# Three PEER stages: score tiles behind the key products and into the gates, wide one-hot compares on VectorE, the weight multiplied in by GpSimd

## The reference

```python
def block(xt):
    q = (xt @ w_q).reshape(T, PEER_HEADS, 2, PEER_HALF)
    s = jnp.einsum('thpd,hpkd->thpk', q, sub_keys)
    s_top, i_top = lax.top_k(s, PEER_TOPK)
    cand = s_top[:, :, 0, :, None] + s_top[:, :, 1, None, :]
    cand_id = i_top[:, :, 0, :, None] * PEER_NKEYS + i_top[:, :, 1, None, :]
    best, pos = lax.top_k(cand, PEER_TOPK)
    eid = jnp.take_along_axis(cand_id, pos, axis=-1)
    gate = jax.nn.softmax(best, axis=-1)
    act = gelu(jnp.einsum('td,thkd->thk', xt, u_tab[eid]))
    return jnp.einsum('thk,thkd->td', gate * act, v_tab[eid])
```

## Time and profile before

| | |
|---|---|
| median of 3 runs | 4071.81 us (4068.31 to 4077.5) |
| the profiled execution, its own time | 4068.67 us |
| its span in the profile | 4066.9 us |
| TensorE busy (modelled) | 87% |
| VectorE, ScalarE, GpSimd busy | 57%, 34%, 11% |
| mean granted TensorE clock | 0.921 of full speed |

### The profile page before, as it was taken

How to read it: one execution, slowest core, us unless ns; L and a number is a source line. 1 busy time by engine, 2 the same in 40 slices (tenths; PEclk the granted TensorE clock), 3 DMA queues, 4 the chain that set the end, 5 groups by cost and what they waited for, 6 DMA issues and landing times. The chain is left out here.

```text
span 4066.9 us, 58259 instructions
## 1 busy us (share of the span) xinstructions
PE 3554.5 (87%) x20168; PEld 2950.0 (73%) x20168; DVE 2324.1 (57%) x4790; ACT 1370.9 (34%) x2097; POOL 427.4 (11%) x460
## 2 busy tenths in 40 slices
PE   7888999999866879999999748797678789999996
PEld 3677899999733667999999627575336779999993
DVE  1488666666314688666666263433205886666662
ACT  1136444444110246444444111111202464444442
POOL 0156000000000274000000000000001650000000
PEclk9999999999987999999999857677789999999998
DMA  4311555555330412555555300000134125555552
GB/s 182 146 57 53 186 186 186 186 187 188 135 127 11 151 52 79 190 186 186 187 187 187 114 0 1 1 1 25 53 118 150 53 69 190 186 186 186 186 186 95
DMA packets 126699, 511.64 MB, mean 126 GB/s; under 512 B 14704, under 2 KB 15344, under 8 KB 119152
## 3 DMA queue, kind: packets, MB, share of 16 engines
q1 hardware_dynamic: 126576, 510.07, 35.0%
HBM read 508.96 MB, written 1.05 MB: 125 GB/s over the span
## 5 line engine op out<-in xcount | busy, mean ns | idle before, releaser
L381 PE MATMUL ps<-xh,uhigh 128*128 128x256 f32 x3072 | 870.5, 283 | 14.7 <-POOL ulow L763 14.7
L383 PE MATMUL ps<-xh,ulow 128*128 128x256 f32 x3072 | 869.2, 283 | 0.0
L382 PE MATMUL ps<-xl,uhigh 128*128 128x256 f32 x3072 | 869.1, 283 | 0.0
L381 PEld LDWEIGHTS ps<-xh,uhigh 128*128 128x128 f32 x3072 | 588.1, 191 | 32.7 <-POOL ulow L763 19.8
L382 PEld LDWEIGHTS ps<-xl,uhigh 128*128 128x128 f32 x3072 | 588.2, 191 | 13.0
L383 PEld LDWEIGHTS ps<-xh,ulow 128*128 128x128 f32 x3072 | 588.1, 191 | 0.0
L728 DVE TENSOR_TENSOR ulow<-stream,uhigh 128x1024 fp32r<-128x1024 f32 x330 | 404.4, 1225 | 184.7 <-ACT uhigh L506 175.1
L506 ACT CAST uhigh<-stream 128x1024 fp32r<-128x1024 f32 x336 | 353.0, 1051 | 413.6 <-DMA stream<-in_u 413.6
L399 PE MATMUL ps<-vhigh,chigh 128*128 128x512 f32 x1536 | 479.7, 394 | 1.8 <-DVE vlow L744 1.5
L399 PE MATMUL ps<-vlow,chigh 128*128 128x512 f32 x1536 | 475.9, 391 | 0.0
L399 PE MATMUL ps<-vhigh,clow 128*128 128x512 f32 x1536 | 474.5, 390 | 0.0
(11 more groups left out here) (347 smaller groups left out, 4050.7 us busy)
## 6 DMA issues: line engine op xcount, KB each, us to landing
stream<-in_u SPq DMA_DIRECT2D x384, 512.0 KB, 4.0
stream<-in_v SPq DMA_DIRECT2D x369, 512.0 KB, 3.3
big<-in_wq SPq DMA_DIRECT2D x24, 1152.0 KB, 7.6
stream<-in_ab_w_in SPq DMA_DIRECT2D x4, 2048.0 KB, 9.1
stream<-in_c_w_qf SPq DMA_DIRECT2D x16, 512.0 KB, 3.4
stream<-in_c_w_ig SPq DMA_DIRECT2D x4, 2048.0 KB, 7.8
stream<-in_w_gates SPq DMA_DIRECT2D x4, 2048.0 KB, 8.3
spare<-in_v SPq DMA_DIRECT2D x15, 512.0 KB, 3.3
```

The lines of the kernel that those rows point to most:

```text
L381: pe.matmul(out, uh[:, b, cols], c.xh[:, k, :], start=k == 0, stop=False)
L382: pe.matmul(out, uh[:, b, cols], c.xl[:, k, :], start=False, stop=False)
L383: ins = pe.matmul(out, ul[:, b, cols], c.xh[:, k, :], start=False, stop=k == KD - 1)
```

## The change

HELD stays 16; EARLY = 24 score tiles are now made ahead of the loop, and the loop has STEPS = 104. Lines of the changed kernel are given as the diff has them.

- *Selection*: four score tiles after round 1's key products, two after round 2's, none after round 3's, ten after the residual product. GpSimd's picks now stand ahead of the low halves of the same round.
- *Gates*: VectorE makes A for two quads with one compare without the weight (128x1024), and B for two quads (128x1024) or, every other time, for one (128x512); ScalarE makes B of every fourth quad. GpSimd multiplies the weight into A of every quad (one tensor_tensor of 128x512) and makes no B. The products go round 3 banks, 4 to 6, and `gate_held` does two quads in one go. Score tiles 16 to 23 are made between the quads, one in 8 quads, into bank 7; their Gelu goes into eight places `late`. Seven of VectorE's low halves (for score tiles 18 to 24) stand in the gates, one after the held outputs have begun.
- *Held outputs*: 24 instead of 16. Three of the `late` places lie in `spare`, so only two slots of v are loaded ahead. VectorE multiplies the eight late tiles by their gates, four after each of the first two.

```diff
+EARLY = 24
+POOL_LOW = 18
-    STEPS = NKEYS - HELD
+    STEPS = NKEYS - EARLY
-    MAKER = "DPAPAPAP"
+    AFTER = {1: range(0, 4), 2: range(4, 6)}
...
+            def gate_scores(g):
+                n, x = HELD + g // 8, g % 8
+                if x == 7:
+                    return
+                if x == 0:
+                    low_done(pe, n)
+                    pe.wait_ge(early_gelu, n)
+                for k in range(0 if x == 0 else x + 1, x + 2):
+                    ins = score_block(early_bank(n), n % 2, k)
+                if x == 6:
+                    ins.then_inc(early_used, 1)
...
-                for n in range(4 * r - 4, 4 * r):
+                for n in AFTER.get(r, ()):
                     early_scores(n)
...
-            for n in range(HELD - 4, HELD):
+            for n in range(6, HELD):
                 early_scores(n)
...
             for g in range(QUADS):
                 b = g % 4
                 pe.wait_ge(a_ready, g + 1)
-                if MAKER[g % 8] == "A":
-                    pe.wait_ge(act_b_ready, made(g))
-                elif MAKER[g % 8] == "P":
-                    pe.wait_ge(b_ready, made(g))
-                if g < 4:
-                    if b >= 2:
-                        pe.wait_ge(early_gelu, HELD - 3 + b)
+                if b == 3:
+                    pe.wait_ge(act_b_ready, g // 4 + 1)
                 else:
-                    pe.wait_ge(dve_moved, g - 3)
+                    pe.wait_ge(b_ready, 2 * (g // 4) + b // 2 + 1)
+                if g < 3:
+                    if g == 2:
+                        pe.wait_ge(early_gelu, HELD - 1)
+                else:
+                    pe.wait_ge(dve_moved, g // 2 - (g % 2 == 0))
                 for q in range(4):
-                    ins = pe.matmul(c.ps[:, 4 + b, q * P:(q + 1) * P], A[:, b, q, :], B[:, b, q, :],
+                    ins = pe.matmul(c.ps[:, 4 + g % 3, q * P:(q + 1) * P], A[:, b, q, :], B[:, b, q, :],
                                     start=True, stop=True)
                 ins.then_inc(g_ready, 1)
+                gate_scores(g)
...
-            for g in range(QUADS):
-                if g >= 4:
-                    dve.wait_ge(g_ready, g - 3)
-                if MAKER[g % 8] == "D":
-                    dve.tensor_tensor(B[:, g % 4], bc(c.iota, 1, 4), bc(c.selt[:, 1, 4 * g:4 * g + 4], 2, P), ALU.is_equal)
-                for q in range(4):
-                    t = 4 * g + q
-                    ins = dve.tensor_scalar(A[:, g % 4, q, :], c.iota[:], c.selt[:, 0, t:t + 1], c.selt[:, 2, t:t + 1],
-                                            ALU.is_equal, ALU.mult)
-                ins.then_inc(a_ready, 1)
-                if g >= 2:
-                    gate_held(g - 2)
+            def one_hot(out, side, g, n):
+                return dve.tensor_tensor(out[:, g % 4:g % 4 + n].rearrange("p b q a -> p (b q) a"), bc(c.iota, 1, 4 * n),
+                                         bc(c.selt[:, side, 4 * g:4 * g + 4 * n], 2, P), ALU.is_equal)
+
+            for x in range(QUADS // 2):
+                g = 2 * x
+                if x >= 2:
+                    gate_held(x - 2)
+                one_hot(A, 0, g, 2).then_inc(hot_ready, 1)
+                one_hot(B, 1, g, 2 if x % 2 == 0 else 1).then_inc(b_ready, 1)
+                if x % 4 == 1 and x >= 5:
+                    late_low(POOL_LOW + x // 4 - 1)
...
+                if n < 2:
+                    for m in range(4 * n, 4 * n + 4):
+                        m = EARLY - HELD - 1 - m
+                        dve.tensor_tensor(G[:, :, m], G[:, :, m], late[m], ALU.mult).then_inc(weighed, 1)
+                if n == 1:
+                    late_low(EARLY + 1)
...
-            early_low(0)
-            early_low(1)
-            for r in range(ROUNDS - 1):
-                early_low(4 * r + 2)
-                early_low(4 * r + 3)
-                pick(r)
-                early_low(4 * r + 4)
-                early_low(4 * r + 5)
-            for n in range(HELD - 2, HELD + 2):
+            for n in range(4):
                 early_low(n)
-            alone(selt_ready, 1)
+            pick(0)
+            early_low(4)
+            early_low(5)
+            pick(1)
+            early_low(6)
+            early_low(7)
+            pick(2)
+            for n in range(8, POOL_LOW):
+                early_low(n)
+            alone(selt_ready, 2)
             for g in range(QUADS):
-                if MAKER[g % 8] != "P":
-                    continue
-                if g >= 4:
-                    alone(g_ready, g - 3)
-                for q in range(4):
-                    t = 4 * g + q
-                    ins = pool.tensor_scalar(B[:, g % 4, q, :], c.iota[:], c.selt[:, 1, t:t + 1], None, ALU.is_equal)
-                ins.then_inc(b_ready, 1)
+                if g % 2 == 0:
+                    alone(hot_ready, g // 2 + 1)
+                pool.tensor_tensor(A[:, g % 4], A[:, g % 4], bc(c.selt[:, 2, 4 * g:4 * g + 4], 2, P), ALU.mult
+                                   ).then_inc(a_ready, 1)
```

More of the change, by code:

```diff
@@ L234, in peer @@
     QW = KD * P
-    STEPS = NKEYS - HELD
+    STEPS = NKEYS - EARLY
     QUADS = T // 4
-    MAKER = "DPAPAPAP"
-    made = lambda g: sum(MAKER[x % 8] == MAKER[g % 8] for x in range(g + 1))
+    AFTER = {1: range(0, 4), 2: range(4, 6)}
     def sem(n):
@@ L295, in peer, with loop_bank, low_done @@
     held_v = [v[:, 0], v[:, 1], c.spare]
-    actv = c.aux[:, 4 * T:6 * T].rearrange("p (b t) -> p b t", b=2)
-    def early_bank(n):
-        return c.ps[:, 6 + n % 2, 0:T]
+    actv = c.aux[:, 0:2 * T].rearrange("p (b t) -> p b t", b=2)
+    late = [actv[:, 0], actv[:, 1]] + [c.extra[:, n * T:(n + 1) * T] for n in range(3)] + [
+        c.spare[:, n * T:(n + 1) * T] for n in range(3)]
+    held_slot = [n if n < 2 else (n - 2) % 3 for n in range(EARLY)]
+    held_turn = [held_slot[:n].count(held_slot[n]) for n in range(EARLY)]
+    held_last = lambda n, b: max(x for x in range(n) if held_slot[x] == b)
+    def early_bank(n):
+        return c.ps[:, 6 + n % 2 if n < HELD else 7, 0:T]
+    def loop_bank(b):
+        return c.ps[:, 7 - 2 * b, 0:T]
+    def low_done(eng, n):
+        if n < POOL_LOW:
+            eng.wait_ge(early_ul, n + 1)
+        else:
+            eng.wait_ge(late_ul, n + 1 - POOL_LOW)
     def steps(eng, body):
@@ L327, in _ @@
             early(3)
-            for n in range(3):
+            for n in range(2):
                 sp.dma_start(held_v[n], v_dram[n]).then_inc(held_v_landed[n], 16)
@@ L464, in body @@
                 outputs(i, b)
-            pe.wait_ge(dve_moved, QUADS - 2)
+            pe.wait_ge(early_gelu, EARLY)
             scores(0, 0, False)
-            for n in range(HELD):
+            pe.wait_ge(dve_moved, QUADS // 2)
+            for n in range(EARLY):
                 pe.wait_ge(held_c, n + 1)
@@ L509, in early_act @@
                 act.wait_ge(early_used, n + 1)
-                act.activation(held[:, n, :], early_bank(n), ACT.Gelu).then_inc(early_gelu, 1)
-                if n + 2 < HELD:
+                out = held[:, n, :] if n < HELD else late[n - HELD]
+                act.activation(out, early_bank(n), ACT.Gelu).then_inc(early_gelu, 1)
+                if n + 2 < EARLY:
                     early_high(n + 2)
                 else:
-                    u_high(0, n + 2 - HELD, False)
+                    u_high(0, n + 2 - EARLY, False)
             act.copy(c.xh, c.xt).then_inc(xh_ready, 1)
@@ L557, in held_high @@
                     act.wait_ge(held_vl, n - 1)
[L558 removed]
+                act.copy(vh[:, n % 2], held_v[b]).then_inc(held_vh, 1)
             def body(i, b, again, ahead):
@@ L712, in _, with gate_held @@
-            gate_held(QUADS - 2)
-            gate_held(QUADS - 1)
-            dve.wait_ge(dve_moved, QUADS)
-            for n in range(HELD):
+            def gate_held(x):
+                dve.wait_ge(act_moved, 2 * x + 2)
+                for g in (2 * x, 2 * x + 1):
+                    part = held[:, :, 4 * g:4 * g + 4].rearrange("p j t -> p t j")
+                    ins = dve.tensor_tensor(part, part,
+                                            c.ps[:, 4 + g % 3, :].rearrange("p (q j) -> p q j", q=4)[:, :, 0:HELD],
+                                            ALU.mult)
+                ins.then_inc(dve_moved, 1)
@@ new lines, in _ @@
+            for x in range(QUADS // 2):
[6 more added lines that the diff above has]
+                    late_low(POOL_LOW + x // 4 - 1)
+            gate_held(QUADS // 2 - 2)
+            gate_held(QUADS // 2 - 1)
+            dve.wait_ge(dve_moved, QUADS // 2)
+            for n in range(EARLY):
@@ L717, in _ @@
                 if n >= 2:
                     dve.wait_ge(held_v_used, n - 1)
-                link(dve.tensor_copy(ch[:, n % 2], held[:, n, :]))
-                dve.tensor_tensor(cl[:, n % 2], held[:, n, :], ch[:, n % 2].bitcast(F32), ALU.subtract
+                part = held[:, n, :] if n < HELD else G[:, :, n - HELD]
```

(7 more changed lines are left out.)

103 lines of the change are left out of this document (55 added, 48 removed).

## The result

| | before | changed |
|---|---|---|
| median (lowest to highest) | 4071.8 us (4068.3 to 4077.5) | 4130.9 us (4130.6 to 4134.4) |
| the profiled execution, its span | 4068.7, 4066.9 us | 4134.4, 4132.6 us |
| mean granted TensorE clock | 0.921 | 0.914 |

The changed kernel takes 1.0146 times as long (95%: 1.0128 to 1.0163): 59 us more by the medians, 66 by the two profiled executions. It is slower, as forecast, and inside the range. The forecast said 80 us, so 14 to 21 us of cost didn't appear.

A forecast was written before the change was run, and what follows sets the result against it. TensorE was taken to bound loop and held outputs, with three engines near the limit in the gates; per stage +48.2 - 23.0 + 4.5 - 3 = +26.7, three stages +80, giving 4152 us, between 4105 and 4222.

The forecast's parts named there:

- Taking turns: Gates: two-SBUF-input instructions of VectorE and GpSimd block each other, each exchange giving back 0.16 us.
- The size of the gates: Gates part of a stage: 145 us against 96.8, +48 us (+37 to +68).
- the floor: Gates: 154.3 us of instructions alone less 20.5 for 128 exchanges, 133.8 us.
- the reserve: Gates: what was added above 133.8 us for waits, taking 145, halfway to 154.3.
- the ring: Gates: chain of waits from multiply through product and copy to compare; as a rival, gates beyond 165 us, 4%.
- The line through L790 and L763: Gates: GpSimd's 128x512 multiply put at 1.36 us, kept for the upper end of 165 us.
- they pass each other: Gates, rival: multiplies leave VectorE alone, gates 95 us, -23 us a stage, kernel 4002; 10%.
- What each instruction would show: Gates profile: L847 at 1.9 us or more, L756 of 1024 above 2, L742 0.27, both engines busy nearly throughout.
- Score tiles: Eight tiles moved from loop to gates: -23.0 us a stage, loop still 5.62 us a step.
- The two gaps on TensorE: Start of held outputs: TensorE loses 1.6 and 2.9 us, +4.5 us a stage (3 to 6).
- The selection: VectorE's 3.82 us wait for a pick goes, ten score tiles after the residual are late next; -3 us (-6 to -1).
- The clock: Gates, rival: TensorE falls to 1.2 GHz, part 185 us, +67 a stage, kernel 4272; 5%; forecast thought it stays.

The follow-up runs named there:

- Experiment 3: experiment 2's kernel with the table iota copied to a free PSUM bank, where VectorE's compares read it; 4132.3 us, 1.0144 of the kernel before.
- (5): The changed kernel with compares no longer waiting for ScalarE's copies and each quad's bank freed by itself; 4119.6 us, 1.0125 of the kernel before.
- experiment 1: The changed kernel with GpSimd's weight multiply in the gates left out; 4065.8 us, 0.9991 of the kernel before.
- (6): Experiment 3 with the looser waits of (5) added; 4060.1 us, 0.9976 of the kernel before.
- experiment 2: The changed kernel without the eight late score tiles (16 ahead of the loop, 112 in it); 4183.1 us, 1.0280 of the kernel before.
- experiment 4: The kernel before with only the eight late score tiles and new selection order, one-hot rows made the old way; 4051.6 us, 0.9954.
- experiment 10: experiment 4 with weighings spread, the last two v loads swapped and the gates' seven low halves moved to GpSimd; 4042.8 us, 0.9927 of the kernel before.

## Why the prediction was right, and where its sizes were off

**Taking turns: right.** Forecast was that a two-operand multiply of GpSimd and a two-operand compare of VectorE exclude each other. VectorE and GpSimd together in the changed kernel's gates:

```profile
340.22 1.85 POOL L847 TENSOR_TENSOR stream<-stream 128x512 f32<-128x512 f32 x1 [1.26 <-DVE stream L756]
341.45 1.70 DVE L756 TENSOR_TENSOR stream<-consts,stream 128x1024 f32<-128x1024 f32 x1
342.04 2.02 POOL L847 TENSOR_TENSOR stream<-stream 128x512 f32<-128x512 f32 x1
343.08 1.52 DVE L756 TENSOR_TENSOR stream<-consts,stream 128x512 f32<-128x512 f32 x1
```

The first multiply ends at 342.07 and the second at 344.06. Between these ends lie 1.99 us for one compare (1.21 alone) and one multiply (1.04 alone): two exchanges gave back 0.26 us, 0.13 each, where the earlier trace rows had shown 0.16. Experiment 3 shows the cause: one operand in PSUM, and both last as long as alone. The rule of the Trainium skill (SBUF — State Buffer, "Who interferes with whom") agrees about who blocks whom; by it nothing would come back, and these two would take 2.25 us, not 1.99.

**The size of the gates: 42 for 48.** The term that was mis-sized is the multiply. Half of L763, 1.19 us, was taken; alone it lasts 1.04 (experiment 3, and the shortest L847 is 1.034). 64 x 0.15 = 9.6 us come off every sum: 144.7 all alone, and 144.7 - 128 x 0.13 = 128 as the floor. The part took 138.8, 11 above this floor, as the forecast lay 11 above its own. That the reserve was right in size is luck: it stood for the ring alone, and loosening the ring gave back 3 us (5). The steps of two quads that hold a stretch at the lower clock, 23 in the three stages, are together 7 us a stage longer than steps at the same places without one. Whether the clock made them longer is not shown. The estimate of 1.12 us from the Trainium skill's GPSIMD Engine Reference ("Elementwise — side-by-side cycle accounting") was nearer than the half of L763, and still high. The line through L790 and L763, the upper end, was the worst of the three.

**The ring was undervalued as a mechanism.** The forecast named the chain from multiply to product to copy to `gate_held` to compare, but let it act only above a floor made of busy times, and would have called a part below 118 us proof against taking turns. The runs show it as a bound of its own: 118 us without any turns in experiment 3, 96 when it is loosened (6). The rival "they pass each other" gave 95 us and a kernel of 4002. It would have been wrong even if its mechanism were true: with the turns gone and the ring left, the kernel of experiment 1 takes 4066. Its 95 us for the gates needed the looser ring of experiment 6.

**What each instruction would show: two misses.** Groups over the gates of the changed kernel:

```profile
L847 POOL TENSOR_TENSOR stream<-stream 128x512 f32<-128x512 f32 x64 | 106.3, 1688 | 28.1 <-DVE stream L756 28.1
L480 PE MATMUL ps<-stream 128*128 128x128 f32 x512 | 79.7, 304 | 33.9 <-POOL stream L847 33.6
L756 DVE TENSOR_TENSOR stream<-consts,stream 128x1024 f32<-128x1024 f32 x48 | 67.0, 1425 | 0.0
L589 ACT COPY big<-ps 128x448 f32<-128x448 f32 x64 | 33.9, 529 | 63.6 <-PE ps L480 63.6
L756 DVE TENSOR_TENSOR stream<-consts,stream 128x512 f32<-128x512 f32 x16 | 23.5, 1471 | 0.0
```

The multiply was to average 1.9 us or more and has 1.69; the compare of 1024 above 2 us and has 1.43. The turns fell on the multiply, 0.65 us each, 42 us in all. The 48 compares lose only 0.21 each: at their start GpSimd is often idle, waiting for just this compare. The 16 short ones, started while a multiply runs, take 1.47 instead of 0.69. GpSimd and VectorE were to be busy nearly all of the part and were so for 77% and 84% of it. `gate_held` kept its 268 ns, as forecast; its second operand is in PSUM.

**Score tiles: right.** The eight tiles went into these slow gates without a price (experiment 2; beside the faster old ones they and what came with them cost 15 us, experiment 4), and left the loop, whose step stayed the same. Held outputs and loop changed by -17.4 to -18.8 us for -18.5. The two gaps on TensorE at the start of the held outputs, with VectorE's L777 ahead of each:

```profile
421.09 0.28 DVE L777 CAST chigh<-big 128x256 fp32r<-128x256 f32 x1
423.11 0.70 PE L436 MATMUL ps<-vhigh,chigh 128*128 128x512 f32 x2 [0.97 <-DVE vlow L781]
...
426.20 0.28 DVE L777 CAST chigh<-big 128x256 fp32r<-128x256 f32 x1
428.23 0.87 PE L436 MATMUL ps<-vhigh,chigh 128*128 128x512 f32 x2 [2.14 <-DVE vlow L781]
```

0.97 and 2.14 us, foretold as 1.6 and 2.9. Some of what they are short came in elsewhere: from its first held output to its first score matmul of the loop TensorE took 44.3 us for 16 tiles before and takes 71.5, 70.1 and 70.2 for 24 now, 5.3, 3.9 and 3.9 us more than eight times 2.74. In the first stage a stretch at the lower clock lies in it (mean 0.50 from 428.6 to 432.0 us).

Of the loop's first Gelu distance, 8.8 us instead of 6.0, only a part is lost time. ScalarE, before and now:

```profile
419.25 1.28 ACT L564 ACT_TABLE_LOAD   x1
420.55 0.39 ACT L564 ACTIVATE stream<-ps 128x256 f32<-128x256 f32 x1
423.77 1.05 ACT L572 CAST vhigh<-stream 128x1024 fp32r<-128x1024 f32 x1 [2.83 <-DMA stream<-in_v]
```

```profile
486.36 0.37 ACT L607 ACTIVATE stream<-ps 128x256 f32<-128x256 f32 x1
...
491.19 1.05 ACT L615 CAST vhigh<-stream 128x1024 fp32r<-128x1024 f32 x1 [4.46 <-DMA stream<-in_v]
...
495.13 0.38 ACT L607 ACTIVATE stream<-ps 128x256 f32<-128x256 f32 x1
```

The table load that stood ahead of the first Gelu is gone from here, since late Gelus already ran in the gates. So this Gelu comes some 1.3 us earlier and the wait for the same load is longer, 4.46 for 2.83 us. TensorE has score matmuls to do meanwhile: from the loop's first score tile to its second it takes 5.86, 7.02 and 5.97 us instead of 5.62, a loss of 0.2, 1.4 and 0.4.

**The selection: right, for the reason given.** The wait of 3.82 us of the earlier trace rows is gone, and what was named as late next took its place:

```profile
265.92 2.35 DVE L657 TENSOR_REDUCE stream<-big 128x64 f32<-128x1024 f32 x2
...
278.33 0.42 DVE L726 TENSOR_REDUCE big<-stream 128x16 f32<-128x256 f32 x1 [10.07 <-ACT stream L572]
```

```profile
277.89 0.42 ACT L572 ACTIVATE stream<-stream 128x256 f32<-128x256 f32 x1
```

VectorE was through at 268.3 and waited 10.07 us for Exp, which starts at 277.89 and not at 272.69: the ten score tiles behind the residual product now pace this end.

**The clock: right as a bound, wrong in detail.** The rival had it fall for the whole part, 185 us; the forecast said it stays. It stood at 1.2 GHz for some 25 us of each gates part (0.91 on average) instead of 6, and for 48 in experiment 2 (0.83). Up to 7 of the 11 us above the floor go along with it.

## What to carry to other kernels

Before giving a second engine part of an elementwise chain, count the SBUF inputs of both engines' instructions: VectorE and GpSimd with two each add up nearly whole, and moving one input to PSUM separates them without any other edit. Follow the waits round the slots too, since the two bounds hide each other: removing one of them gave 3 or 19 us here, removing both 41 (2 to 6). Look at the granted clock before comparing two runs of one part: it differed by 0.14 between experiments 2 and 3. And measure a change of two halves by halves: here one gave -19 us alone and the whole +59.

## What the runs showed of the hardware, unexpected

- GpSimd's two-operand instruction isn't linear from 1024 elements downward: 1.04 us for 128x512 with a broadcast second operand, 2.36 to 2.38 for 128x1024 subtractions. The size, the operand's form and the output's type differ here; which of them makes it cheap was not separated.
- A VectorE compare with iota in PSUM lasts as long as with iota in SBUF and GpSimd idle: 1.213 us on average (3) and 1.215 (1).
- A narrow VectorE `tensor_scalar` with one tensor input is hardly held up by GpSimd's narrow one-input instructions (327 to 472 ns, median 335, in experiment 4), but for up to 2.39 us by a two-input one of 2.36 us (experiment 10).
